# A decoder layer with product-key experts on one core: two token parts become three, with z and retention columns kept in DRAM

## The reference

```python
z = rms_norm(x, g_mix)
rq, rk, rv, aq, ak, av, ga, gb = jnp.split(z @ w_in, IN_SPLITS, axis=-1)
# rotations of rq, rk (retention) and aq, ak (attention)
r_out, r_state = ret_fn(rq, rk, rv, log_decay)          # 4 heads, 128 x 256, chunks of 128 tokens
a_out = att_fn(aq, ak, av, lam)                         # 4 heads, softmax 1 - lam * softmax 2, causal
m = jax.nn.sigmoid(ga) * (r_out @ w_br_ret) + jax.nn.sigmoid(gb) * (a_out @ w_br_att)
h = x + m @ w_out
z2 = rms_norm(h, g_ffn)
# peer: 8 heads, product keys over 128 x 128 single-neuron experts, top 16 of each head
sc = jnp.einsum('thcd,hcnd->thcn', (z2 @ w_query).reshape(T, 8, 2, 128), sub_keys)
ids, gate = top 16 of the sums of the two halves' top 16, softmax of their sums
act = gelu(einsum('thkd,td->thk', expert_u[ids], z2)) * gate
h = h + einsum('thk,thkd->td', act, expert_v[ids])
```

## Time and profile before

| | |
|---|---|
| time, median of 3 runs | 4201.55 us (4199.16 to 4207.85) |
| the profiled execution, its time | 4203.96 us |
| its span, first to last instruction | 4202.1 us |
| TensorE busy (matmul) | 3194.1 us, 76% |
| VectorE busy | 2589.5 us, 62% |
| ScalarE / GpSimd busy | 670.5 / 1294.6 us |
| moved by DMA | 1002.69 MB, 239 GB/s over the span |
| gathers of the lookup, software queue | 687.91 MB |

### The profile page before, as it was taken

One profiled execution on the slowest core, in us unless ns is written; L12 is line 12 of the kernel. 1 busy time (PEld: TensorE's weight loads), 2 busy tenths in 40 slices (PEclk: granted clock), 3 DMA queues, 4 the chain that ended last, 5 costly groups with the idle time before them and its releaser, 6 DMA issues. The chain is left out here.

```text
span 4202.1 us, 32255 instructions
## 1 busy us (share of the span) xinstructions
PE 3194.1 (76%) x10192; PEld 1860.9 (44%) x10192; DVE 2589.5 (62%) x5283; ACT 670.5 (16%) x1711; POOL 1294.6 (31%) x930
## 2 busy tenths in 40 slices
PE   6998988998884644754465333698999899999995
PEld 3553435774562412322233333355555555555553
DVE  2221134001598864689569877487778778787876
ACT  1110012001112401122110333011111111111111
POOL 0000000000133232366323555244444444444442
PEclk9999975999995666877787666799999999999997
DMA  4002000112213597799741366899999999999996
GB/s 133 0 1 71 25 11 35 53 53 108 68 36 138 188 339 255 319 416 418 283 164 30 124 254 252 333 413 384 388 401 416 384 403 400 395 407 409 405 376 254
DMA packets 265660, 1002.69 MB, mean 239 GB/s; under 512 B 26306, under 2 KB 117458, under 8 KB 180242
## 3 DMA queue, kind: packets, MB, share of 16 engines
q0 software_dynamic: 95728, 687.91, 40.4%
q1 hardware_dynamic: 164370, 304.30, 20.1%
q10 hardware_dynamic: 5392, 8.42, 0.5%
HBM read 952.70 MB, written 47.85 MB: 238 GB/s over the span
## 5 line engine op out<-in xcount | busy, mean ns | idle before, releaser
L198 POOL DMA_INDIRECT lk_rows<-in_expert_uv,lk_ids x640 | 1031.6, 1612 | 1369.3 <-DVE lk_sums L239 1269.6
L239 DVE SCALAR_TENSOR_TENSOR lk_sums<-lk_rows,lk_weights,lk_sums 128x1024 f32<-128x1024 f32 x647 | 829.8, 1283 | 38.6 <-DVE lk_sums L239 1.4
L1963 PE MATMUL ps<-zT_B,ex_u 128*128 128x384 f32 x2048 | 716.0, 511 | 171.5 <-DMA ex_u<-in_expert_uT 171.5
L208 DVE SCALAR_TENSOR_TENSOR lk_rows<-lk_rows,lk_z_rows 128x1024 f32<-128x1024 f32 x648 | 772.6, 1223 | 62.3 <-DMA lk_rows<-in_expert_uv,lk_ids 57.6
L1976 PE MATMUL ps<-ex_a,ex_v 128*128 128x384 f32 x2048 | 672.4, 489 | 27.5 <-DVE accT L2011 16.5
L1963 PEld LDWEIGHTS ps<-zT_B,ex_u 128*128 128x128 f32 x2048 | 407.3, 200 | 474.8 <-DMA ex_u<-in_expert_uT 191.4
L1976 PEld LDWEIGHTS ps<-ex_a,ex_v 128*128 128x128 f32 x2048 | 389.7, 191 | 305.1 <-DVE accT L2011 26.3
L216 ACT ACTIVATE lk_weights<-lk_weights 128x2 f32<-128x2 f32 x324 | 66.0, 204 | 1792.8 <-DVE lk_rows L208 1792.6
L1560 POOL MEMSET rtA_scores<- 128x128 f32 x2 | 0.4, 204 | 1014.5 <-POOLq L86 1014.5
L2011 DVE TENSOR_TENSOR accT<-accT,ps 128x384 f32<-128x384 f32 x248 | 128.3, 548 | 268.7 <-PE ps L1976 268.7
L1871 PE MATMUL ps<-ga_onehot_i,ga_onehot_j 128*128 128x128 f32 x768 | 104.6, 299 | 145.4 <-issue 94.9
(11 more groups left out here) (379 smaller groups left out, 3647.8 us busy)
## 6 DMA issues: line engine op xcount, KB each, us to landing
ex_u<-in_expert_uT SPq DMA_DIRECT2D x128, 512.0 KB, 14.3
ex_v<-in_expert_v SPq DMA_DIRECT2D x128, 512.0 KB, 11.6
gate_scratch<-ga_stage SPq DMA_DIRECT2D x3, 8192.0 KB, 68.0
ex_gates<-gate_scratch SPq DMA_DIRECT2D x128, 192.0 KB, 8.5
mgA_w<-in_w_merge SPq DMA_DIRECT2D x8, 1792.0 KB, 7.4
mgB_w<-in_w_merge SPq DMA_DIRECT2D x8, 1792.0 KB, 11.0
lk_rows<-in_expert_uv,lk_ids POOLq DMA_INDIRECT x640, 10.9
w_ret<-in_w_ret SPq DMA_DIRECT2D x4, 2048.0 KB, 18.4
```

The source lines that it names most:

```text
L198: pool.indirect_dma_start(out=self.slot[:, s, :], out_offset=None, in_=self.a["expert_uv"], in_offset=bass.IndirectOffsetOnAxis(ap=index, ...
L208: self.nc.vector.scalar_tensor_tensor(out=u, in0=u, scalar=1.0, in1=self.z[:, t % 2, :], op0=ALU.mult, op1=ALU.mult, accum_out=self.w[:, t ...
L239: self.nc.vector.scalar_tensor_tensor(out=total, in0=v, scalar=w, in1=total, op0=ALU.mult, op1=ALU.add).then_inc(self.added, 1)
L1963: last = nc.tensor.matmul(ps[:, n % HB, 0:DENSE], U[:, n % UB, k, :], zD[:, k, :], start=(k == 0), stop=(k == KD - 1))
```

## The change

The nine tiles come in three parts: A tiles 0 and 1 (FIRST = 2), B tiles 2 to 4, C tiles 5 to 7 and the samples. Each runs attention, merge, residual and routing; the lookup begins with part B's attention. The transposed z of parts B and C is stored to DRAM in the projection stage, their retention columns tile by tile in the retention stage, and both are loaded again at the start of the part's attention. The samples' projected rows go by way of DRAM too. `PER` of the merge is 3 batches a step. The lookup has 7 row buffers. The key pages are laid out as channel, head, position (2 KB runs). Routing holds four weight buffers for two. The gate stage stages half tiles of 64 tokens in two buffers (runs of 256 B) with 2 batches after each. The expert stage holds five buffers of expert_u and four of gates. The residual stage writes its squares over x, and its w_out tiles belong to a scope of their own, `OutWeights`.

```diff
-LT = 5
+FIRST, LT = 2, 5
...
-    SLOTS = 8
+    SLOTS = 7
...
-        A, B = Half("A", TILES[:LT]), Half("B", TILES[LT:])
+        A, B, C = parts = [Part(0, TILES[:FIRST]), Part(1, TILES[FIRST:LT]), Part(2, TILES[LT:])]
...
+        for p in parts:
+            lookup = look if p is not A else None
+            attention_phase(nc, a, ps, ident, mem, p, late.get(p), KT, VA, lam, lookup)
+            if p is C:
+                sample_phase(nc, a, ps, ident, mem, p, rows_s, lam, look)
+            with OutWeights(nc, a, mem, p) as w_out:
+                merge_phase(nc, a, ps, mem, p, w_out, lookup)
+                residual_phase(nc, a, ps, ident, mem, p, w_out, h_dram, z_dram, lookup)
+            routing_phase(nc, a, ps, ident, mem, p, look, picks if p is C else None, gs_dram, is_dram)
...
@@ retention_phase
+            for t in range(FIRST, NT):
+                p = of_tile[t]
+                sp.wait_ge(kept, ONE + t + 1)
+                sp.dma_start(p.columns(p.r_kept, t), columns[:, t % 2, :, :]).then_inc(r_stored[t % 2], 16)
...
@@ attention_projection
+            for p in later:
+                sp.dma_start(p.z_kept, p.z[:, :, :]).then_inc(kept_back, 16)
+            sp.dma_start(rows_s["rqk"], s_rqk[:, :]).then_inc(kept_back, 16)
+            sp.dma_start(rows_s["rv"], s_rv[:, :]).then_inc(kept_back, 16)
...
@@ attention_phase
+            if late:
+                half.z, half.r = late
+                sp.dma_start(half.z[:, :, :], half.z_kept).then_inc(s_late, 16)
+                sp.dma_start(half.r[:, :, 0:P * M], half.r_kept[:, :, 0:P * M]).then_inc(s_late, 16)
+                sp.wait_ge(s_late, ONE + 32)
...
@@ sample_phase
+            for n, buf in (("rqk", s_rqk), ("aqk", s_aqk), ("rv", s_rv), ("av", s_av)):
+                sp.dma_start(buf[:, :], rows_s[n]).then_inc(s_rows, 16)
...
-                                 a["cache_kT"][ds(page(b, pg), 1)].rearrange("o h p n -> p (o h) n")
+                                 a["cache_kT"][ds(page(b, pg), 1)].rearrange("o p h n -> p (o h) n")
...
+            pe.wait_ge(s_rows, ONE + 64)
...
+            dve.wait_ge(s_rows, ONE + 64)
...
@@ merge_phase
-        PER = -(-7 // nb)
+        PER = 3 if nb == 1 else 2
...
@@ residual_phase
-                    sp.wait_ge(added[u], ONE + it)
+                    sp.wait_ge(squared[u], ONE + it)
...
-                nc.scalar.activation(junk[0:rows, :], h[0:rows, u, :], ACT.Square,
+                nc.scalar.activation(x[0:rows, u, :], h[0:rows, u, :], ACT.Square,
...
@@ routing_phase
-        wq = sb("wq", [P, 2, KD, P])
+        WB = 4
+        wq = sb("wq", [P, WB, KD, P])
...
@@ gate_phase
-        PER = P // GT
+        HT = P // 2
+        PER = HT // GT
         SETS = 3
-        BETWEEN = 8
+        BETWEEN = 2
+        stage = sb("stage", [P, 2, NK, HT])
...
-                if tile and local == 0:
-                    act.wait_ge(out, ONE + 16 * tile)
+                if part >= 2 and local == 0:
+                    act.wait_ge(out[part % 2], ONE + 16 * (part // 2))
...
+            for n in range(2 * DT):
+                sp.wait_ge(kept, ONE + PER * (n + 1))
+                sp.dma_start(g_dram[:, :, n * HT:(n + 1) * HT].rearrange("i j t -> j i t"),
+                             stage[:, n % 2, :, :]).then_inc(out[n % 2], 16)
...
@@ expert_phase
-    UB, GB = 3, 3
+    UB, GB = 5, 4
```

More of the change, by code:

```diff
@@ L117, in place, with __init__ @@
         return self.nc.alloc_sbuf_tensor_at(name, list(shape), dt, offset=lo)
-class Half:
-    def __init__(self, name, tiles):
-        self.name, self.tiles = name, tiles
+class Part:
+    def __init__(self, index, tiles):
+        self.name, self.tiles = "ABC"[index], tiles
+        self.att, self.sample, self.merge, self.res, self.route = range(3 + 5 * index, 8 + 5 * index)
         self.lo, self.width = tiles[0][1], sum(r for _, _, r in tiles)
@@ L305, in build @@
[L305 to L311, removed]
+        z_C = mem.place("zT_C", [P, KD, C.width], C.att, EXPERTS)
@@ new lines, in build @@
+        KT = mem.place("KT", [P, AH, SEQ], PROJ, C.att)
+        VA = mem.place("VA", [P, NT, AH * ADV], PROJ, C.att)
+        A.z = mem.place("zT_A", [P, KD, A.width], NORM, A.route)
+        A.r = mem.place("rT_A", [P, KD, A.width], RET, A.merge)
+        for p in reversed(parts):
+            p.q = mem.place(f"qT_{p.name}", [P, AH, P * len(p.whole)], PROJ, p.att)
+            p.a = mem.place(f"aT_{p.name}", [P, AH, p.width], p.att, p.merge)
+            p.m = mem.place(f"mT_{p.name}", [P, KD, p.width], p.merge, p.res)
@@ L462, in retention_phase @@
         turned, kept, stored = sem("out_turned"), sem("out_kept"), sem("stored")
+        columns = sb("columns", [P, 2, KD, P])
+        r_stored = [sem(f"columns_stored{u}") for u in range(2)]
         ACT_V, PROJ = 3, WR // BANK
@@ L988, in sb @@
         def sb(n, shape, dt=F32):
-            return mem.place("sa_" + n, shape, SAMPLE, dt=dt)
+            return mem.place("sa_" + n, shape, half.sample, dt=dt)
         def sem(n):
@@ L1261, in _, with __init__, load, merge_phase @@
                                     gain[:, 0:1], 1.0 - LAM_INIT, ALU.mult, ALU.mult).then_inc(a_kept, 1)
-def merge_phase(nc, a, ps, mem, half, stage, look):
+class OutWeights(Scope):
+    def __init__(self, nc, a, mem, half):
+        super().__init__(nc)
+        self.a = a
+        self.cols = [mem.place(f"w_out{half.name}{b}", [P, KD, BANK], half.res) for b in range(2)]
+        self.loaded = [self.queue_sem(f"w_out_loaded{half.name}{b}") for b in range(2)]
+        self.callback(self.zero)
+    def load(self, sp, b):
+        sp.dma_start(self.cols[b][:, :, :], self.a["w_out"][:, :, b * BANK:(b + 1) * BANK]).then_inc(self.loaded[b], 16)
+def merge_phase(nc, a, ps, mem, half, w_out, look):
     NW = 2 * KD + KD + AH
@@ L1270, in sb @@
         def sb(n, shape):
-            return mem.place(f"mg{half.name}_{n}", shape, stage)
+            return mem.place(f"mg{half.name}_{n}", shape, half.merge)
         def sem(n):
@@ L1824, in gate_phase @@
             "onehots_i_ready", "onehots_j_ready", "weighed", "products_done", "kept"))
-        out = sem("stored")
-        steps = range(DT * PER)
+        out = [sem(f"stored{u}") for u in range(2)]
+        steps = range(2 * DT * PER)
         block = ctx.block()
```

183 lines of the change are left out of this document (91 added, 92 removed).

## The result

The changed kernel takes 4080.0 us (median of 4 runs, 4074.11 to 4082.75) against 4204.7 us (4199.16 to 4207.92) for the kernel before beside it: a ratio of 0.9703, 95% interval 0.9686 to 0.972. The forecast was 4105, in a range of 4045 to 4178. The profiled execution has a span of 4081.0 us.

What follows compares the result with a forecast made beforehand. A lookup batch costs VectorE 5.0 and DMA 5.2 us, so stages given too many are paced by batches. Terms +6, +59, -141, +46, +38, -28, -83, +3, +4 sum to -96: 4204 to 4108, median 4105, range 4045 to 4178.

Steps and rivals of the forecast that it cites:

- the signs that were named: Merges about 168 us, routings 479, gates without idle DMA stretches, sample periods 16 us, experts within 15 us of 1511.
- Batches: Lookup batches ahead of the experts: 118 for 120, so the expert stage has two batches more.
- Merge, -121 for -141: Merges of parts A, B and C: 108, 168 and 170 us, sum 446 for 587; B bound by DMA at 407 GB/s.
- Attention, residual, routing, stores: Stages rebuilt in three parts: attention +59, residual +46, routing +38, retention and projection with the last small stores +6 us.
- my allowance of 32 us for start and tail: Part B's attention: 32 us added to VectorE's 106 for idle time and short steps waiting on each other, making 138.
- Samples, 0 for -28: Sample stage: key pages in 2 KB runs cut the period from 21.4 to 16 us; with 4 us lost, -28.
- Gates, -109 for -83: Gate stage: half tiles in two buffers at 35.5 us each, 256 B writes at 24.6 ns; 231 us for 314.
- The first rival: Gate store: 256 B writes cost double a packet, gates 384 to 426 us, whole 4258 to 4300; chance 0.11.
- Experts, -20 for +3: Expert stage: deeper buffers -10 because DMA engines are already full, two batches and five gathers more +13; sum +3 us.
- That the split does nothing by itself: Attention, residual and routing pay 143, merges return 141; without gates and samples nil, 4216 if both stay; chance 0.03.
- The partial-overlap rival: Merge steps take 22 us, not 20: merges give back 32, part B's attention 12, residual 10, routing 12; 4171; chance 0.22.
- The "more is hidden" rival: 256 B packets at 19 ns put gates at 198 us, experts take -25, samples run at 14 us: 4048; chance 0.20.

Runs made afterwards that it cites:

- two parts: Kernel before, no third part, with 3 batches a merge step, half-tile gates with 2 batches each, five and four expert buffers: ratio 0.9779.
- the last version but one: Changed kernel with state reads ahead of the next sample's scores, 2 batches a step in attention C, 3 a tile in residual stages: ratio 0.9615, 4042.39 us.
- The move on TensorE's queue: Changed kernel with the state reads of sample b - 1 put ahead of the score products of sample b: ratio 0.965.

## Why the prediction was right, and where its terms were off

*The way and the size held.* Measured 4080 against 4105. The step that carried it, that a batch costs 5.0 to 5.2 us on VectorE and DMA alike and that stages are paced by what is hung on them, was right: 5.3 us a batch in merges and gates. In the expert stage it was less even: 4.5 (two parts), 5.5 (the last version but one) and 5.6 to 6.3 (four batches a merge step) with deep buffers, 3.7 at most with the old ones.

*How near the total came is in part luck.* Samples and merge missed by 28 and 20 us one way, gates, experts and attention by 26, 23 and 17 the other; the 25 us are what is left of these.

*Of the signs that were named,* the gate stage without idle DMA stretches came, the routings add up to 475 for 479, part B's stages took 552 us for 556, and a half tile's store landed in 29.5 us, under 45. The merges took 178 and 177 us at DMA share 0.91 and 0.92, not 168 at 0.97; the samples' period was 22 us, not 16; the experts moved by 20 us, outside the 15 that were named and inside the 30.

*Batches.* 118 for 120 was right, and the expert stage's gain did not come from fewer of them.

*Merge, -121 for -141.* Right in its bound, mis-sized. 8 batches more cost 39 and 46 us, about their price in bytes. The 65 MB stand, but they moved at 381 GB/s and not 407 for the first 166 us of merge B, and in its last 13 us no engine computes while the last gathers land, where the sum had 8 us for start and end together. Row buffers are part of it: part C's merge took 177.2 us with seven, the same merge 171.7 and 173.5 with eight, and 193.4 with six.

*Attention, residual, routing, stores.* Part B's attention took 128 for 138, part A's 43 for 49, the residual stages and routing were within 5 us. VectorE is busy 105.4 us in attention B, as added up (106); my allowance of 32 us for start and tail was 10 too large. Four weight buffers gained nothing in routing, as forecast: part C's took 197.1 us to the gate stage's first instruction, and 196.6 with two in the kernel before.

*Samples, 0 for -28.* The step that failed is the subtraction of the issue and landing times from the period. The issue did fall, from 7.1 to 3.6 us, but the key pages land no sooner, 9.3 us for 8.1. The 3.4 us to landing that were taken for runs of 2 KB are the median of 32 value pages, and 24 of these are issued behind the loop, with fewer gathers beside them (DMA share 0.57 from 1650 to 1712 us). The kernel before has 8 in the loop, of the same size and runs, and they took 7.4 us, where the key pages took 8.1. Its value pages at 1470 to 1640 and at 1650 to 1712 us:

```profile
sa_value_pages<-in_cache_v SPq DMA_DIRECT2D x8, 256.0 KB, 7.4
...
sa_value_pages<-in_cache_v SPq DMA_DIRECT2D x24, 256.0 KB, 3.0
```

Besides, SP asks for the next sample only when TensorE has passed this one's scores. The move on TensorE's queue shows this second cause. The first rests on the landing times; that it is the gathers in front that hold the pages up wasn't tried by itself.

*Gates, -109 for -83.* The mechanism was right and the price of a 256 B write too high: 15 to 19 ns for 24.6, so a half tile takes 30.1 us, VectorE's and DMA's at once, for 35.5. The first rival is refuted. (The gates of 327 us that it was to decide at belong to 40 ns a packet and not 41; nothing hangs on it.)

*Experts, -20 for +3.* The step "the DMA engines are already full, -10" failed in size. The deeper buffers are worth 48 us on the kernel before and 35 to 46 on the changed one, by which of its three traces is taken. Share 0.97 was not full: going to 0.99 came with 3% more bytes a second.

*The rivals.* That the split does nothing by itself was nearer the truth than its chance of 0.03: with samples at 0 and gates and experts taken out, the rebuilt stages are 10 us longer. But they carry 10 batches more in that time, 53 us at 5.3 each, and two parts with all the rest are 29 us slower. So of 125 us some 30 are the split's, with the loss of a row buffer counted in, and the others belong to the gates' double buffer, the buffers of the expert stage and the evened merge. These three alone, on the kernel before, gave about 52, 50 and 35 us, and together (in the run with two parts, with 12 batches fewer in the gates) 93. So their gains don't add. That they fill the same gaps in the DMA engines is the likely reason: the second and the third each took the expert stage's share from 0.97 to 0.99. It was argued and not tried in pairs. The partial-overlap rival fell as a whole, though the merges took 20 of its 32 us; its attention, residual and routing came out under the forecast. The "more is hidden" rival held for gates and experts and not for the samples.

Open: what the change from 8 to 7 row buffers costs alone, and what the split is worth with 8. These weren't run.

## What to carry to other kernels

When work that can be hung anywhere costs the same bytes everywhere, moving it gains only where the receiving stage has idle DMA; a DMA share of 0.97 still hides some 3%, and the cheap way to it was here a prefetch as deep as the consumer's burst. In an in-order load queue a load that is asked for one step earlier waits for a later event and holds every load behind it, so when buffer counts change, check which event each load waits for, and not only how far ahead it is. And a chain "ask, land, compute, ask" is broken by the order on the computing engine as well as by more buffers: two buffers were there, and only one was ever in flight. A landing time is worth only what the traffic beside it was: one median over a busy loop and a quiet end misled the sum for the samples.

## What the runs showed of the hardware

- Stores from SBUF to DRAM, alone on 16 DMA engines: 256 B packets 15.2 to 18.6 ns each, 512 B packets 24.6 to 28.0. Both sizes show two levels within one store.
- Lookup with six, seven row buffers of 8 KB a partition: 374 and 398 GB/s in the expert stage; one buffer was worth 131 us of the whole. A buffer was held 22.1 and 24.2 us.
- One gate row (192 KB) asked for one step earlier by SP, with three buffers: +361 us in the expert stage, 9% of the kernel.
- Loads of 256 KB in runs of 2 KB (value pages, kernel before) landed in 7.4 us beside gathers and in 3.0 in a stretch of DMA share 0.57.
